# Prompt attention on one core: one reciprocal for the sums of two units, and a unit normalised three slots behind its score in place of two

## The reference, cut to what matters

```
p = masked_softmax(q @ k.T * scale - slopes * dist, mask)
o = g[..., 0] * o_c + g[..., 1] * (p_s @ v_sel) + g[..., 2] * (p_w @ v_w)
```

## Time and profile before

| | |
|---|---|
| median of 3 runs | 1059.06 us (1058.37 to 1059.9) |
| the profiled execution: time, span | 1058.09 us, 1056.0 us |
| mean granted TensorE clock | 0.955 of full speed |
| busy over the span | PE 93%, DVE 62%, ACT 38%, POOL 37% |
| the prompt attention | first score at 758.04 us, last one at 921.52 us of the span |

### The profile page before, as it was taken

How to read it: one execution, slowest core, us unless ns; L and a number is a source line. 1 busy time by engine, 2 the same in 40 slices (tenths; PEclk the granted TensorE clock), 3 DMA queues, 4 the chain that set the end, 5 groups by cost and what they waited for, 6 DMA issues and landing times.

```text
span 1056.0 us, 19270 instructions
## 1 busy us (share of the span) xinstructions
PE 986.1 (93%) x7168; PEld 836.4 (79%) x7168; DVE 649.7 (62%) x1399; ACT 404.6 (38%) x794; POOL 386.6 (37%) x328
## 2 busy tenths in 40 slices
PE   2999999999999959999899998999699999999996
PEld 0989998998899729998799678999577777756684
DVE  4498999899989679320751312344888888833103
ACT  5333334333334276221331111244577777711001
POOL 2487888788878658001010000000333333100000
PEclk9999999999999959999899999998799999999796
DMA  8243453355334450360255015211630000260002
GB/s 342 75 128 101 127 174 103 101 139 163 101 105 137 139 202 1 120 238 7 115 152 133 1 26 221 80 61 41 205 124 1 0 1 1 104 235 1 1 1 85
DMA packets 43016, 108.01 MB, mean 102 GB/s; under 512 B 20674, under 2 KB 21730, under 8 KB 38530
## 3 DMA queue, kind: packets, MB, share of 16 engines
q1 hardware_dynamic: 42946, 106.99, 31.2%
HBM read 81.87 MB, written 12.17 MB: 89 GB/s over the span
## 4 chain that ended last, share of the span: by engine, by line
PE 82%; DVE 7%; issue 4%; ACT 4%; POOL 3%; DMA 0%; DVEq 0%; ACTq 0%
PE ps L567 52%; PE ps L953 7%; PE ps L593 4%; PE ps L843 4%; POOL C L1737 3%; PE ps L731 2%; PE ps L831 2%; PE ps L939 1%; PE ps L545 1%; DVE SX L1527 1%; DVE KL L1496 1%; PE ps L820 1%; PE ps L795 1%; DVE X L1263 1%; PE ps L822 1%
## 5 line engine op out<-in xcount | busy, mean ns | idle before, releaser
L567 PE MATMUL ps<-Hh,ringAh 128*128 128x256 f32 (+1 forms) x768 | 161.2, 291 | 14.3 <-DVE X L1263 14.3
L567 PE MATMUL ps<-Hh,ringAl 128*128 128x256 f32 (+1 forms) x768 | 159.4, 289 | 0.0
L1307 DVE SCALAR_TENSOR_TENSOR acc<-VP,tapc,acc 128x512 f32<-128x512 f32 x122 | 159.1, 1304 | 0.0
L567 PE MATMUL ps<-Xl,ringAh 128*128 128x256 f32 (+1 forms) x768 | 158.1, 287 | 0.0
L1706 POOL TENSOR_TENSOR ringAl<-ringA,ringAh 128x1024 fp32r<-128x1024 f32 x48 | 121.1, 2535 | 73.3 <-ACT ringAh L1029 73.2
L567 PEld LDWEIGHTS ps<-Hh,ringAh 128*128 128x128 f32 x768 | 123.3, 189 | 27.2 <-DVE X L1263 14.6
L567 PEld LDWEIGHTS ps<-Xl,ringAh 128*128 128x128 f32 x768 | 124.1, 189 | 0.0
L567 PEld LDWEIGHTS ps<-Hh,ringAl 128*128 128x128 f32 x768 | 123.0, 189 | 0.0
L1307 DVE SCALAR_TENSOR_TENSOR ps<-VP,tapc,ps 128x512 f32<-128x512 f32 x138 | 102.8, 745 | 0.6
L843 PE MATMUL ps<-PTB,V 128*128 128x512 f32 (+3 forms) x256 | 91.0, 439 | 2.5 <-ACT PTB L1206 2.1
L567 PE MATMUL ps<-Hh,ringEh 128*128 128x256 f32 (+1 forms) x384 | 84.2, 302 | 7.1 <-DVE ringEl L1373 4.6
(11 more groups left out here) (233 smaller groups left out, 2059.6 us busy)
## 6 DMA issues: line engine op xcount, KB each, us to landing
ringA<-in_w_a SPq DMA_DIRECT2D x16, 1536.0 KB, 7.3
G<-VP SPq DMA_DIRECT2D x60, 260.0 KB, 4.8
ringE<-in_w_f SPq DMA_DIRECT2D x24, 512.0 KB, 3.6
ringC<-in_w_c SPq DMA_DIRECT2D x8, 1024.0 KB, 5.9
cache_cmp<-in_cache_cmp SPq DMA_DIRECT2D x32, 128.0 KB, 2.8
cache_sel<-in_cache_sel SPq DMA_DIRECT2D x16, 256.0 KB, 3.0
cache_win<-in_cache_win SPq DMA_DIRECT2D x1, 4096.0 KB, 15.2
out_win_s<-in_win_state SPq DMA_DIRECT2D x1, 4032.0 KB, 18.1
```

What stands on the lines that cost most here:

```text
L567: mm = nc.tensor.matmul(dst, w, x[:, cols], start=begins, stop=ends)
L1307: nc.vector.scalar_tensor_tensor(tap_sum(k % 2), src, w, tap_sum(k % 2), ALU.mult, ALU.add).then_inc(conv_step, 1)
```

## The change

VectorE inverts the sums of two units with one instruction (two columns instead of one), in even slots alone, and a unit is normalised in the third slot behind its score. The semaphore of the reciprocal counts pairs. The copy of the gates moves from slot 1 to slot 2 of a pair, and the tail after the last pair has one unit more.

```diff
             def invert(i, u):
 
-                dve.wait_ge(exp_ready, 16 * i + u + 1)
-                nc.vector.reciprocal(gsc[:, u:u + 1], rsum[:, u:u + 1]).then_inc(inv_ready, 1)
+                dve.wait_ge(exp_ready, 16 * i + u + 2)
+                nc.vector.reciprocal(gsc[:, u:u + 2], rsum[:, u:u + 2]).then_inc(inv_ready, 1)
 
             def normalize(i, u):
 
                 r, b, t = u // 8, u % 8 // 4, u % 4
                 if u == 0:
                     dve.wait_ge(gate_set, i + 1)
-                dve.wait_ge(inv_ready, 16 * i + u + 1)
+                dve.wait_ge(inv_ready, 8 * i + u // 2 + 1)
                 w = weights_at(u)[:, 0:(t + 1) * P]
...
             def attend(i):
                 for u in range(16):
                     score(i, u)
-                    if u >= 2:
-                        normalize(i, u - 2)
+                    if u >= 3:
+                        normalize(i, u - 3)
                     elif reaches(i, 1):
-                        normalize(i - 1, u + 14)
-                    if u >= 1:
-                        invert(i, u - 1)
-                    elif reaches(i, 1):
-                        invert(i - 1, 15)
-                    if u == 1:
+                        normalize(i - 1, u + 13)
+                    if u % 2 == 0:
+                        if u >= 2:
+                            invert(i, u - 2)
+                        elif reaches(i, 1):
+                            invert(i - 1, 14)
+                    if u == 2:
                         set_gates(i)
...
+            normalize(7, 13)
+            invert(7, 14)
             normalize(7, 14)
-            invert(7, 15)
             normalize(7, 15)
```

## The result

The changed kernel takes **1151.54 us** (median of 4 runs, 1143.04 to 1152.6), against 1059.48 us for the kernel before on the same chip. The ratio is 1.083 (95% interval 1.078 to 1.089). The profiled execution took 1151.13 us, and its span of 1149.2 us is 93.2 us longer than that of before. The forecast was 1152 us. Beside the experiments over a third of the executions of the kernel before took 1064 to 1069 us and the rest 1056 to 1061, so that the ratios given there, which agree with means over both, stand some 0.3% lower than beside the rest alone.

A forecast was written before the change was run, and what follows sets the result against it. TensorE was taken to set the pace before, a closed ring with VectorE after: 32.5 us a pair against 21.0, eight pairs 92 us, plus 1 for the tail, on 1058.1, and 1 for the median: 1152 us, range 1134 to 1178.

The forecast's parts named there:

- The ring: Prompt attention: score, normalisation, transposes, next product, next score wait in turn without slack; 1.50 to 2.39 us a slot against 1.31.
- from the weight load of the transposes to L822: TensorE's transposes and L820 before the second score matmul (L822): 0.28, 0.49, 0.71, 0.92 us for t = 0 to 3.
- The thirds: Interpolation for t = 1 and 2 between 0.28 and 0.92 us, from transposes' weight load to L822: 0.49 and 0.71.
- the first rival: TensorE's clock falls as well, low half of the time: 35.7 us a pair, 25 us more in all, 1177 us; chance 0.18.
- the likeliest case: The closed ring alone in the prompt attention, at 32.5 us a pair against 21.0: 1152 us, chance 0.78.
- L822 to the score: From the second score matmul to VectorE's score start: 0.33, 0.33, 0.39, 0.44 us for t = 0 to 3.
- the compressed slot: Slot with the compressed product, twice a pair: TensorE alone needs 2.22 us to the next L822, against the ring's 1.50.
- the hand-over through a register instruction: Score's wait in the rolled loop, units 0 to 6: 0.21 us instead of 0.05, counting in six slots, 1.0 us a pair.
- GpSimd's operation: Stretches a normalisation to 1.40 us from 0.47, each half pair, in the slot with the compressed product; taken as 0.
- The tail's 1 us: Behind the last score, the transposes of unit 12 wait for its normalisation: 1.0 us.
- TensorE's busy share: Sign in the changed profile's attention: 60 to 70% busy at a clock of 1.00.
- Not slower: Rival: VectorE sets the pace, 64 fewer reciprocals give 1049 us; or TensorE stays the bound, 1059; chance 0.04.

The follow-up runs named there:

- Run 2: Kernel before, with each unit normalised in the third slot behind its score and one reciprocal per unit: 1152.98 us, ratio 1.085.
- runs 3: Changed kernel, with the score product ahead of the transposes in TensorE's slot: 1075.1 us, ratio 1.013.
- 5: Changed kernel, with transposes and copies five slots behind the score instead of four and value products nine instead of eight: 1063.68 us, ratio 1.003.
- 8: Changed kernel, with score product ahead of the transposes, transposes and copies five slots behind, value products nine: 1057.62 us, ratio 0.997.
- Run 6: Changed kernel, with 150 products of no use added in TensorE's pauses: 1141.7 us, 9.8 us less than the changed kernel.
- runs 1: Changed kernel, with units normalised two slots behind again, paired reciprocals kept ahead of the normalisation, gate copy back in slot 1: 1061.85 us, ratio 1.0003.
- 7: Kernel before, with score product ahead of the transposes and paired reciprocals, normalised two slots behind: 1055.55 us, ratio 0.995.

## Why the prediction was right

**The ring** was right in place and in kind. Run 2 puts the whole loss on the third slot; runs 3, 5 and 8 cut the ring at TensorE's order, at its distance, and at both, and give back 76, 88 and all of the 92 us.

**Its size was too large.** The forecast had 32.5 us a pair; undisturbed, it is 31.4 (951.57 to 982.92 of after). The mis-sized term is the one from the weight load of the transposes to L822. Taken were 0.28, 0.49, 0.71 and 0.92 us for t = 0 to 3; at full clock with TensorE idle ahead it measures 0.23, 0.40, 0.57 and 0.73 (957.04 to 957.77 above for the last). The 0.92 came from pair 0, and that stretch was not at full clock. The window of the kernel before around it, which the forecast left out of account, has the clock at 0.65:

```profile
760.00:765.00 5.00, 4.78 (x22) 3.89 (x23) 4.08 (x21) 3.98 (x14) 0.38 (x1) 0.65 1.22 443
```

The thirds drawn between 0.28 and 0.92 carried the error on to t = 1 and 2. Over sixteen slots, two of which the compressed product covers, that is 1.7 us a pair too much. About 0.6 us came back in slots that the sum had as plain ones, at the turn from unit 7 to 8 and from 15 to the next pair: 1.96 and 1.99 us in the pair from 951.57 us on, where the sum with 0.23 would have 1.68. There the same term, from the weight load to L822, takes 0.52 and 0.47 us (966.87 to 967.39, and 982.18 to 982.65). The code has waits for other engines between transposes and product in these two slots; that they are what costs is not shown.

**The clock fell too, a little.** It was the first rival, with 3.2 us a pair at half of the time low. It happened, in short stretches (clock of 0.86 and 0.91 over 20 us), and cost 196.28 - 187.70 = 8.6 us over six pairs, 1.4 a pair. So the likeliest case and the rival were not exclusive: the outcome is a mixture, 83 us of ring and 10 of clock, where the forecast had 93 of ring and none of clock. That the two errors cancel is luck. What the Trainium skill says in "TensorE: Matmul & The Clock Gate", section "A second HAM failure mode: psum-queue depth-cycling", of a kernel whose small pauses made the clock swing, the trace bears out; the price that the forecast's working gave it (25 us) the trace does not. Run 6 is the other side of it: with the pauses partly filled the clock stays up.

**The other terms.** Where the forecast read 8.9 us of waiting for score products, it left out the score's own waits, 19.8 us with them; that VectorE has little to wait for before holds all the same. L822 to the score (0.32 to 0.44 us), the scores and normalisations, and the compressed slot were as taken: 2.22 us between L822 at 951.29 and 953.51, as in the earlier trace rows. So was the hand-over through a register instruction: 955.43 + 0.34 = 955.77, and the score starts at 955.97, 0.20 us later; in the slots without it, 0.05. The reciprocal, the copy of the gates and all but 0.1 us of the gate products stayed hidden. GpSimd's operation met the normalisation of the slot with the compressed product, as said, and no more. The tail's 1 us can't be seen beside the clock. TensorE's busy share at full clock is 14.73 / 20 = 74%, where 60 to 70% had been named: the forecast divided the recorded work of a busy stretch by the new length, and more than that is recorded. Why was not pursued; no term of the sum rested on it.

**"Not slower"** fell. What the Trainium skill, "VectorE: DVE Perf Modes", section "Rules for kernel authors", advises, to bring down the number of operations, is no help here, where VectorE doesn't set the pace: runs 1 and 7 do that and gain nothing.

## What to carry to other kernels

Before a step is moved by a slot, write down which instruction of each in-order engine stands behind which, and look for a ring: here 64 fewer instructions came with a closed ring that cost 0.65 us in each of 128 slots. On the engine that waits, put what is ready (the next product) ahead of what is not, or add a slot of distance on the other engine too. And a duration that is to carry a sum is read only where the granted clock has been looked up for that stretch.

## What was not expected of the hardware

A reciprocal of two columns costs what one of one column does. The group of after, which answers to the earlier trace rows:

```profile
L1518 DVE RECIPROCAL gsc<-rsum 128x2 f32<-128x2 f32 x64 | 10.1, 157 | 0.5 <-ACT SX L1197 0.3 <-ACT S L1197 0.2
```

The clock fell in some pairs and not in others that repeat the same instructions: two of the six pairs (31.4 us) lose nothing to a dip, two took over 2 us more. Run 2, which has the same ring, has its long pairs in other places: 31.6, 34.0, 31.1, 31.2, 33.2 and 34.2 us, of which these rows bound the second and the third.

```profile
818.90 1.81 PE ps L839 x2
852.89 0.91 PE ps L839 x2
883.97 0.91 PE ps L839 x2
```

What decides where a dip comes was not explained. And adding work made the kernel faster: 150 products of no use on TensorE took 9.8 us off the time.
